# Expert weights in one DRAM tensor, and 38 of 64 experts a layer in one transfer

## The reference, cut to what matters

```python
scores = sigmoid(h @ w_router)                 # 64 experts, group-limited top 8 per token
gates  = 2.5 * chosen scores / their sum
act    = silu(h @ w_gate[e]) * (h @ w_up[e])   # each expert: 1024 -> 256
routed = sum over e of gates[e] * (act @ w_down[e])     # 256 -> 1024
h      = layer_norm(alpha * h + routed + shared expert)
```

## Time and profile before

| | |
|---|---|
| median of 3 runs | 1526.09 us (1524.43 to 1526.24) |
| profiled execution, its own time | 1527.0 us |
| its span, first to last instruction | 1525.2 us |
| TensorE busy | 1439.5 us, 94% of the span |
| moved by DMA | 512.38 MB, 336 GB/s over the span |
| expert stage of layer 0 | about 400 to 890 us of the span |
| expert stage of layer 1 | about 1036 to 1525 us of the span |
| mean granted TensorE clock | 0.98 of full speed |

### The profile page before, as it was taken

One profiled execution on the slowest core, in us unless ns is written; L12 is line 12 of the kernel. 1 busy time (PEld: TensorE's weight loads), 2 busy tenths in 40 slices (PEclk: granted clock), 3 DMA queues, 4 the chain that ended last, 5 costly groups with the idle time before them and its releaser, 6 DMA issues. The chain is left out here.

```text
span 1525.2 us, 24355 instructions
## 1 busy us (share of the span) xinstructions
PE 1439.5 (94%) x9430; PEld 847.1 (56%) x9430; DVE 648.8 (43%) x1463; ACT 338.3 (22%) x714; POOL 250.3 (16%) x331
## 2 busy tenths in 40 slices
PE   8999998999899899999998999988989999999986
PEld 6888768887555455454453467863434444434422
DVE  2767558632532344344342358063233333333324
ACT  3755454320410111111111030141001111111111
POOL 5779625301100000000000000011000000000000
PEclk9999999899999999999999999999999999999999
DMA  8669462049599999999999984849999999999996
GB/s 286 212 197 229 167 179 76 2 171 383 214 417 425 423 422 425 420 419 418 416 425 422 412 319 154 359 184 371 418 424 424 425 424 422 418 423 421 426 419 249
DMA packets 98832, 512.38 MB, mean 336 GB/s; under 512 B 36996, under 2 KB 38084, under 8 KB 59804
## 3 DMA queue, kind: packets, MB, share of 16 engines
q1 hardware_dynamic: 88892, 481.75, 79.7%
q0 software_dynamic: 9824, 29.05, 5.0%
HBM read 508.85 MB, written 17.10 MB: 345 GB/s over the span
## 5 line engine op out<-in xcount | busy, mean ns | idle before, releaser
L1895 PE MATMUL banks<-upper,e_xgT 128*64 128x512 f32 (+1 forms) x880 | 193.7, 606 | 7.3 <-issue 6.5
L371 PE MATMUL banks<-hT,dense_ring 128*128 128x272 f32 x768 | 183.9, 398 | 5.2 <-DMA dense_ring<-in_w_in 5.2
L1467 POOL DMA_INDIRECT x_xg<-rows_dram,x_idx x54 | 53.5, 991 | 803.5 <-DVE x_idx L1459 781.7
L2108 DVE TENSOR_TENSOR e_ac<-e_sl,banks 128x256 f32<-128x256 f32 x54 | 22.7, 421 | 371.7 <-ACT e_sl L2024 371.7
L1895 PE MATMUL banks<-experts,e_xgT 128*64 128x512 f32 (+1 forms) x720 | 172.6, 611 | 5.7 <-issue 5.4
L371 PEld LDWEIGHTS banks<-hT,dense_ring 128*128 128x128 f32 x768 | 146.7, 192 | 38.6 <-DMA dense_ring<-in_w_in 5.2
L1895 PEld LDWEIGHTS banks<-upper,e_xgT 128*64 128x64 f32 (+1 forms) x880 | 65.1, 130 | 126.9 <-issue 126.9
L1895 PE MATMUL banks<-dense_ring,e_xgT 128*64 128x512 f32 (+1 forms) x288 | 126.8, 593 | 0.0
L2024 ACT ACTIVATE e_sl<-banks 128x256 f32<-128x256 f32 x54 | 20.8, 385 | 472.5 <-PE banks L1895 472.5
L1950 PE MATMUL banks<-dense_ring,e_aT 128*64 128x512 f32 (+1 forms) x304 | 113.3, 611 | 3.4 <-DVE acc L2078 2.8
L1915 PE MATMUL banks<-x_sg,route_consts 128*128 128x272 f32 x432 | 104.3, 393 | 0.5 <-DVE acc L2093 0.5
(11 more groups left out here) (462 smaller groups left out, 2067.6 us busy)
## 6 DMA issues: line engine op xcount, KB each, us to landing
upper<-in_moe_gate_up SPq DMA_DIRECT2D x43, 2048.0 KB, 22.2
experts<-in_moe_gate_up SPq DMA_DIRECT2D x34, 2048.0 KB, 21.7
upper<-in_moe_down SPq DMA_DIRECT2D x43, 1024.0 KB, 17.9
experts<-in_moe_down SPq DMA_DIRECT2D x43, 1024.0 KB, 17.4
dense_ring<-in_moe_down SPq DMA_DIRECT2D x38, 1024.0 KB, 19.4
dense_ring<-in_moe_gate_up SPq DMA_DIRECT2D x18, 2048.0 KB, 21.8
upper<-in_moe_gate_up SPq DMA_DIRECT2D x24, 1024.0 KB, 18.0
dense_ring<-in_w_in SPq DMA_DIRECT2D x47, 512.0 KB, 4.8
```

Source lines behind the costliest of these rows:

```text
L371: mm = pe.matmul(ps[g % 4][:, 0:T], slot[:, n % SLOTS_IN, c, :], hT[:, c, :], start=(c == 0), stop=(c == DC - 1))
L1467: pool.indirect_dma_start(out=ex["xg"][:, i % 2, :], out_offset=None, in_=mem["rows_dram"], in_offset=bass.IndirectOffsetOnAxis(ap=ex["idx ...
L1895: mm = pe.matmul(gub[e * n:(e + 1) * n, :], xgT[:, i % 2, c, e * n:(e + 1) * n], gate_up_weights(mem, j)[:, c, :], start=(c == 0), stop=(c ...
L2108: dve.tensor_tensor(ac[:], sl[:], gub[:, FF:], ALU.mult).then_inc(mul, 1)
```

## The change

The host lays out each expert's gate, up and down weights side by side in one DRAM tensor `moe`, so that the 24 KB that a partition gets lie in one run; before there were two tensors, `moe_gate_up` and `moe_down`. For 38 of the 64 experts of each layer (`WHOLE`: those that units 3 to 23 request, except the six that go to slot 5 and those of `IN_HALVES`) one transfer with 128 runs of 24 KB takes the place of the two. SP issues it at the place where it issued the down transfer, after `dn` of unit i, and no longer after `gu`. The other 26 experts are loaded as before, from the new tensor. `gate_up` of a `WHOLE` expert waits for the whole transfer (semaphore `gate_up_ready`), and `down` waits for nothing more.

By units: unit 3 requests experts 14, 15, 17 whole and 16 in parts; units 4, 5, 7, 8, 10, 11, 13, 14, 16, 17, 19, 21 and 22 request two whole experts; units 6, 9, 12, 15, 20 and 23 one whole and one in parts; unit 18 three whole and one in parts.

```diff
+WHOLE = [j for i in range(SHARED_UNIT + 1, len(UNITS)) for j in LOADS[i]
+         if SLOT_OF[j] < RING - 1 and j not in IN_HALVES and j != SHARED_NEXT]
+IN_PARTS = [j for j in range(E) if j not in WHOLE]
...
 def load_gate_up(sp, k, mem, layer, e, j):
-    sp.dma_start(expert_slot(mem, j)[0], k["moe_gate_up"][layer, e]).then_inc(mem["gate_up_ready"][SLOT_OF[j]], 16)
+    sp.dma_start(expert_slot(mem, j)[0], k["moe"][layer, e][:, 0:GATE_UP]).then_inc(mem["gate_up_ready"][SLOT_OF[j]], 16)
+
+def load_whole(sp, k, mem, layer, e, j):
+    s, dense = SLOT_OF[j], mem["dense"][:].rearrange("p i c n -> p (i c n)")
+    slot = mem["experts"][:, s] if s < 4 else dense[:, 0:SLOT]
+    sp.dma_start(slot, k["moe"][layer, e]).then_inc(mem["gate_up_ready"][s], 16)
...
 def load_down(sp, k, mem, layer, e, j):
-    sp.dma_start(expert_slot(mem, j)[1], k["moe_down"][layer, e]).then_inc(mem["down_ready"][SLOT_OF[j]], 16)
+    sp.dma_start(expert_slot(mem, j)[1], k["moe"][layer, e][:, GATE_UP:]).then_inc(mem["down_ready"][SLOT_OF[j]], 16)
...
-                    else:
+                    elif any(j not in WHOLE for j in js):
                         sp.wait_ge(gu, i + 1)
                         for e, j in zip(es, js):
-                            load_gate_up(sp, k, mem, layer, e, j)
+                            if j not in WHOLE:
+                                load_gate_up(sp, k, mem, layer, e, j)
                     if i == SHARED_UNIT + 1:
                         sp.wait_ge(sh_dn, PIECES)
                         load_down(sp, k, mem, layer, expert_at(sp, mem, SHARED_NEXT), SHARED_NEXT)
                     sp.wait_ge(dn, i + 1)
                     for e, j in zip(es, js):
-                        if j not in LAST_IN:
+                        if j in WHOLE:
+                            load_whole(sp, k, mem, layer, e, j)
+                        elif j not in LAST_IN:
                             load_down(sp, k, mem, layer, e, j)
...
-                        else:
-                            pe.wait_ge(dn_ready[SLOT_OF[j]], times_loaded(layer, j))
+                        elif j in IN_PARTS:
+                            pe.wait_ge(dn_ready[SLOT_OF[j]], times_loaded(layer, j, IN_PARTS))
```

More of the change, by code:

```diff
@@ L1251, in load_gate_up_half @@
     ready = (mem["gate_up_low_ready"], mem["gate_up_ready"])[half][SLOT_OF[j]]
-    sp.dma_start(expert_slot(mem, j)[0][:, part], k["moe_gate_up"][layer, e][:, part]).then_inc(ready, 16)
+    sp.dma_start(expert_slot(mem, j)[0][:, part], k["moe"][layer, e][:, part]).then_inc(ready, 16)
 def load_down_half(sp, k, mem, layer, e, j, half):
@@ L1259, in load_down_half @@
     sp.dma_start(down_weights(mem, j)[:, :, part],
-                 k["moe_down"][layer, e].rearrange("p (c n) -> p c n", c=FC)[:, :, part]).then_inc(ready, 16)
+                 k["moe"][layer, e][:, GATE_UP:].rearrange("p (c n) -> p c n", c=FC)[:, :, part]).then_inc(ready, 16)
 def load_down(sp, k, mem, layer, e, j):
-    sp.dma_start(expert_slot(mem, j)[1], k["moe_down"][layer, e]).then_inc(mem["down_ready"][SLOT_OF[j]], 16)
+    sp.dma_start(expert_slot(mem, j)[1], k["moe"][layer, e][:, GATE_UP:]).then_inc(mem["down_ready"][SLOT_OF[j]], 16)
 EXPERT_CONSTS = ("sort_par", "unit_first", "spread_pos", "slot_id", "tok", "pair_base")
@@ L2228, in item @@
                 w_gate_up, w_down = expert_slot(mem, e)
-                sp.dma_start(w_gate_up, k["moe_gate_up"][layer, p * 2 + e]).then_inc(gu_ready, 16)
-                sp.dma_start(w_down, k["moe_down"][layer, p * 2 + e]).then_inc(dn_ready, 16)
+                sp.dma_start(w_gate_up, k["moe"][layer, p * 2 + e][:, 0:GATE_UP]).then_inc(gu_ready, 16)
+                sp.dma_start(w_down, k["moe"][layer, p * 2 + e][:, GATE_UP:]).then_inc(dn_ready, 16)
         over_items(sp, longest, item)
@@ L3019, in layout @@
     rows = lambda w: w.reshape(DEPTH, E, DC, P, FF).transpose(0, 1, 3, 2, 4)
-    r["moe_gate_up"] = np.concatenate([rows(a["moe_w_gate"]), rows(a["moe_w_up"])], axis=-1).reshape(DEPTH, E, P, GATE_UP)
-    r["moe_down"] = a["moe_w_down"].reshape(DEPTH, E, FC, P, D).transpose(0, 1, 3, 2, 4).reshape(DEPTH, E, P, FC * D)
+    r["moe"] = np.concatenate([
+        np.concatenate([rows(a["moe_w_gate"]), rows(a["moe_w_up"])], axis=-1).reshape(DEPTH, E, P, GATE_UP),
+        a["moe_w_down"].reshape(DEPTH, E, FC, P, D).transpose(0, 1, 3, 2, 4).reshape(DEPTH, E, P, FC * D)], axis=-1)
     rows = lambda w: w.reshape(DEPTH, DC, P, FF).transpose(0, 2, 1, 3)
```

## The result

The changed kernel took 1539.57 us (median of 4 runs, 1533.38 to 1545.74) where the kernel before took 1525.26 in the same session: ratio 1.0088, 95% interval 1.0062 to 1.0115. It is slower, by 14 us and not by the 5 of the forecast, and lies 1.6 us above the range. A second session with the same kernel gave 1537.85 against 1526.09, ratio 1.0067 (1.0043 to 1.0091). The change costs 12 to 14 us.

What follows compares the result with a forecast made beforehand. In the pairs DMA engines and TensorE are both full, TensorE setting the pace; layer 1 ends through a transfer, TensorE close behind. 3.5 + 0.7 + 1 = +5.2 on 1526.1 gives 1531.3, said as 1531, range 1523 to 1538 us.

Steps and rivals of the forecast that it cites:

- (b): SP makes 38 fewer issues a layer, about 0.5 us each: saves nothing; parts read from 24 KB rows: nothing.
- (c): Around unit 3, expert 13's down weights land sooner; TensorE gets 4.5 us ahead from `gate_up(5)` through the pairs.
- (d): Gate and up requests 9.3 us later in pairs; DMA queue dry 2.3 us (layer 1), 1.7 (layer 0) through unit 17.
- (e): `gate_up(24)` waits for all unit 22's bytes: starts +3.7 and +2.9 us, less slack +3.5 (layer 1), +0.7 (layer 0).
- The slack: At each layer's end, how much of a later `gate_up(24)` is absorbed: 0.2 us in layer 1, 2.2 in layer 0.
- Bytes decide: Rival, faster: layer ends stay with the last transfer, so long runs save 9.2 us minus gaps, near 1520; chance 0.13.
- Fixed cost: Rival, faster: 76 fewer transfers each save a fixed cost, 190 us by the row, near 1336; chance 0.01.
- gain nothing: Rival, slower still: 24 KB runs save nothing, unit 24's later start costs 5.5 and 3.5 us, clock 1: 1536; chance 0.14.
- (a): Runs of 24 KB in whole-expert transfers save 0.12 us an expert: 3.0 through unit 16, 4.4 through 22, 4.6 a layer.
- the cover of a single request: Time until everything asked before a request has landed, less request time; under 2.6 us, DMA engines run dry for the difference.
- (f): TensorE's clock after waits: unit 24's longer wait costs as before; new wait before `gate_up(5)` adds 1 us over both layers.

Runs made afterwards that it cites:

- The last two kernels of the group on which whole experts cost: Changed kernel without experts 56, 57 whole: 1533.17 us, 1.0048; also without 42, 43 whole: 1526.91 us, 1.0004.
- Filling the waits: Changed kernel with useless matmuls ahead of the waits of `gate_up` 5, 18 and 24 (second version: 3, 4, 12): 1531.09 us, 1.0029.
- the first filled version: Changed kernel with 8, 8 and 24 useless matmuls ahead of the waits of `gate_up` 5, 18 and 24: 1561.79 us, 1.0224.
- unit 24's four alone: Kernel before with only experts 54 to 57 loaded whole, all others as before: 1537.24 us, 1.0065.
- the wait alone: Kernel before, in which `gate_up(24)` also waits for its experts' down weights: 1534.16 us, 1.0056.

## Why the prediction was wrong

**Right.** The bound was read rightly, and the mechanism named for the loss is the one that is there. (b) holds: 24 KB rows of the new tensor are read in parts at no cost (1.0001). (c) holds and was more: TensorE starts `gate_up(5)` at 101.6 and 100.3 us after the layer's first `gate_up` where it started at 107.8 and 107.0, a lead of 6.2 to 6.7 for a forecast of 4.5. In (d), the bare part holds: 1 MB into an empty queue took 4.8 us, so 2.3 bare beside 2.5 of movement. (The Trainium skill, DMA: Bandwidth & Descriptors, section "Anatomy of one DMA", has about 2.0 for the path of GpSimd; this row and the earlier trace rows have 2.3 and 2.5 for SP's.) In (e) the jump by the wait itself was taken as 5.8 us in layer 1 (1464.2 + 0.3 - 1458.73) and measured alone as 425.4 - 420.1 = 5.3; in layer 0 as 5.6 and measured as 4.4. The slack was 1.5 and 3.0 us (7.6 - 6.1, 4.6 - 1.6) for 0.2 and 2.2. The rivals on the faster side fell. "Bytes decide": unit 22's bytes did not come early. "Fixed cost": nothing is saved by fewer transfers where they queue. On the slower side "gain nothing", at 1536, came nearest by its number; in layer 1 its effect is there, but not its reason, as the next paragraphs show.

**The step that failed is the saving carried through (a) and (d) into (e)**: that unit 22's bytes land 2.7 us earlier in layer 0 and 2.1 in layer 1. Measured, as means of the same profiles, they land 1.0 earlier and 1.7 later, and `gate_up(24)` starts 4.6 and 7.6 us later for 2.9 and 3.7. By stretches, in us against before:

| landing of the last byte asked by | layer 0 | layer 1 | forecast |
|---|---|---|---|
| unit 17 | -2.3 | +1.0 | -1.5 and -0.9 |
| unit 19, less that | +1.8 | +1.35 | -0.6 |
| unit 22, less that | -0.5 | -0.6 | -0.6 |

(The forecast is 0.12 us for each whole expert, 27, 5 and 5 of them, less the gaps of 1.7 and 2.3.) In the last stretch, with a full queue, the 24 KB runs give 0.10 to 0.12 us an expert, as taken. In the middle stretch stands what I did not look for: *a wait before `gate_up(18)`*. Unit 18 is of four experts, as unit 24 is. Its last two are asked by unit 16, one unit's time before, all of them only after `down(16)`, and it now waits for all of their bytes. The number was at hand. Unit 16's bytes landed at 317.9 us after layer 0's first `gate_up` in before and `gate_up(18)` started at 318.2, so with a lead of 4.5 TensorE had to meet them, even with the 3.0 of (a) taken off. Most of the lead of (c) was given back there, the clock fell behind the wait (0.58), unit 18's request came late, and the queue ran dry. I put gaps at units 13 to 17 by the cover of a single request and checked no consumer between units 5 and 24. The last two kernels of the group on which whole experts cost show the size: 42 and 43 in parts take the time from 1.0048 to 1.0004.

In the first stretch, layer 1 lost where it should have gained. Here are 180 us of its pairs, of before, of the kernel with late requests in two transfers and of the changed kernel:

```profile
1170.00:1350.00 180.00, 177.37 (x776) 75.61 (x775) 65.00 (x136) 24.47 (x56) 10.83 (x11) 1.00 1.01 422
1170.00:1350.00 180.00, 174.24 (x764) 73.89 (x760) 63.72 (x132) 24.25 (x55) 10.91 (x11) 1.00 1.01 422
1170.00:1350.00 180.00, 177.37 (x780) 75.43 (x778) 64.68 (x136) 24.41 (x56) 10.88 (x11) 1.00 1.00 420
```

All four profiles of before have 422 GB/s, the five of the changed kernel 420, 417, 415, 415 and 417. At 417 for 422 the same bytes take some 2 us longer. And here is one stretch of 10 us in it, of the changed kernel, then of before (the same new profile as above), then of the kernel with late requests in two transfers:

```profile
1300.00:1310.00 10.00, 10.00 (x49) 3.91 (x46) 1.28 (x5) 0.76 (x2) 0.99 (x1) 1.00 0.93 359
```
```profile
1300.00:1310.00 10.00, 9.76 (x46) 3.81 (x46) 2.89 (x7) 0.96 (x2) 0.99 (x1) 1.00 1.02 431
```
```profile
1300.00:1310.00 10.00, 10.00 (x44) 4.33 (x42) 3.40 (x7) 1.25 (x3) 0.00 (x0) 1.00 1.02 427
```

Only with 24 KB runs are engines idle in the pairs (0.93), at a time when the cover of a request was still 4 to 5 us and not under the 2.6 of (d). Lateness alone does not do it, but it also leaves more cover: 8.7 us at unit 14's request (issued at 1298.46; what was asked before landed at 1307.17). So it is not shown whether the longer runs or the smaller cover let engines run dry. Why some of the 16 engines run out before others was not tried.

**(f) was sized at 1 us and is worth more.** "The longer wait costs the same as before" holds for `gate_up(24)` itself (9.70 us, before 9.93). It does not hold behind it: the stage between the layers costs 2.7 us more, far from any wait that the change touches. Filling the waits gives this view of the price: from the start of `gate_up(24)` to the layer's end 49.4 and 49.2 us instead of 51.3 and 51.6, some 4 us over both layers, and the same 49.4 and 49.2 in the first filled version. The 154.7 for the stage between the layers instead of 159.0 can't be put down to the fill: it is of the fastest of 12 runs, and the first version has 162.9. A fill in the kernel before, whose own wait of 5 to 6 us at unit 24 also halves the clock, was not tried; in the version with four experts a layer in parts it brought 1.0004 to 0.9993, within the intervals.

Against the sum of the prediction: layer 1 +6.1 for +3.5, layer 0 +1.6 for +0.7, the rest +3.0 for +1. That makes 10.7 of the 12 to 14 measured; five single profiles do not sample the spread of the runs (1531 to 1546) well, and the remainder is not assigned.

**What stays open.** The prices do not add up: unit 24's four alone +11, the wait alone +7.5 to 8.6, unit 18's +6, all together 12 to 14. And the stage between the layers is not tied to the wait by one rule. The kernel with late requests in two transfers waited 9.01 and 9.95 us at unit 24 and had 0.83 in the stretch above and 155.0 us for the stage, while the profiled run of the version with 42, 43, 56 and 57 in parts had a wait of 4.86, a clock of 0.66 and 160.7 us. So the clock there is shown to be lower on the mean of the changed kernel's profiles, but what in a run makes it fall there is not. That the whole loss goes back to waits of TensorE is thus shown for the expert stages (7.7 of 10.7 us) and open for the rest.

## What to carry to other kernels

When two transfers become one, every consumer of the first part inherits the wait of the second, and if the one is asked for where the second was, the first part is late as well. Walk through all of them, not the known late one alone: compare each start with the landing of its last byte, less the lead won elsewhere. A unit that uses twice the weights is such a place each time it comes. Price a wait of TensorE by the clock behind it as well, and compare the later stages over several profiles of each kernel: here the stage without any change differed by 2.7 us on the mean. And fewer, longer transfers save nothing where transfers already stand in a queue at full rate.

## What the runs showed of the hardware

- A float32 matmul with 128 rows of 512 columns and 128 columns of weights costs 0.88 us (24 records of half of it in 10.57 us).
- A kernel can become faster by work that is thrown away: 1.0067 to 1.0029, with `gate_up(24)` at a granted clock of 1.00 in 7.07 us for 8.5 to 9.9.
- Single runs of either kernel spread by some 15 us: 1531 to 1546 over 11 timed runs of the changed one, 1519 to 1535 over 24 of the kernel before in the second session. Three of them, profiled one by one, order by the clock of the whole run: 1536.08 at 0.977, 1538.08 at 0.974, 1542.34 at 0.970.
- With 24 KB runs the 16 DMA engines were 7% idle in a stretch in which transfers were waiting, with 4.9 us of cover, and moved 415 to 420 GB/s over 180 us; with 16 and 8 KB runs at the same lateness, and more cover, they were not, and moved 422.
